# Issuing the merge stage's branch weights from SyncE, round by round, instead of from ScalarE at the stage's head

## The reference

```python
gates = jax.nn.sigmoid(pg.astype(jnp.float32)).astype(dt).reshape(B, T, N_BRANCHES, D_MODEL)
merged = (gates[:, :, 0] * (o_a.astype(dt) @ w_branch_a)
          + gates[:, :, 1] * (o_b.astype(dt) @ w_branch_b)
          + gates[:, :, 2] * (o_c.astype(dt) @ w_branch_c))
x = x + merged @ w_out
u = rmsnorm(x, norm_ffn) @ w_up
...
x = x + (jax.nn.silu(gate) * val) @ w_down
```

## Time and profile before

| what | value |
|---|---|
| time, median of 3 runs | 2480.94 us (2479.97 to 2484.48) |
| the profiled execution's own time | 2482.44 us |
| span of the profiled execution, first to last instruction | 2480.8 us |
| mean granted TensorE clock over the span | 0.948 |
| PE busy | 2253.4 us (91%) |
| DVE busy | 1195.8 us (48%) |
| POOL busy | 673.1 us (27%) |
| ACT busy | 438.8 us (18%) |

### The profile page before, as it was taken

The page is one execution under the profiler, slowest core; times in us unless marked ns, Lnnn a source line. Parts: engine busy times, 40 slices in busy tenths (PEclk is TensorE's granted clock), DMA queues, the critical chain, the costliest instruction groups (busy, mean ns, idle before and its releaser), DMA issues. The chain is left out here.

```text
span 2480.8 us, 46397 instructions
## 1 busy us (share of the span) xinstructions
PE 2253.4 (91%) x19177; PEld 2058.7 (83%) x19177; DVE 1195.8 (48%) x1735; ACT 438.8 (18%) x693; POOL 673.1 (27%) x622
## 2 busy tenths in 40 slices
PE   4999999999999899987787697999999999999986
PEld 3999999888888888864356466989999999999975
DVE  2343443455553143327955262187527735752743
ACT  4001111111110021125743130130000100000022
POOL 3211112333342200002520022334223323432333
PEclk6999999999999999978988798999999999999998
DMA  6112334878885400026662343111111111111113
GB/s 164 49 45 77 133 108 160 260 249 270 261 266 175 163 4 4 4 100 203 224 247 91 115 149 119 43 35 43 41 50 46 39 40 51 43 41 45 47 44 108
DMA packets 256398, 270.14 MB, mean 109 GB/s; under 512 B 24044, under 2 KB 230869, under 8 KB 254508
## 3 DMA queue, kind: packets, MB, share of 16 engines
q1 hardware_dynamic: 214896, 191.93, 24.5%
q10 hardware_dynamic: 33212, 53.18, 6.3%
q0 software_dynamic: 8080, 22.06, 2.6%
HBM read 219.83 MB, written 69.11 MB: 116 GB/s over the span
## 5 line engine op out<-in xcount | busy, mean ns | idle before, releaser
L135 PE MATMUL ps<-ml,fu_wh 128*128 128x352 f32 (+1 forms) x1248 | 410.4, 329 | 22.9 <-POOL fu_wl L129 17.8
L135 PE MATMUL ps<-xl_a,ap_wh 128*128 128x352 f32 (+2 forms) x1200 | 404.7, 337 | 12.4 <-POOL ap_wl L129 12.4
L137 PE MATMUL ps<-mh,fu_wl 128*128 128x352 f32 (+1 forms) x1248 | 409.2, 328 | 0.0
L136 PE MATMUL ps<-mh,fu_wh 128*128 128x352 f32 (+1 forms) x1248 | 409.0, 328 | 0.0
L136 PE MATMUL ps<-xh_a,ap_wh 128*128 128x352 f32 (+2 forms) x1200 | 397.0, 331 | 0.0
L137 PE MATMUL ps<-xh_a,ap_wl 128*128 128x352 f32 (+2 forms) x1200 | 396.7, 331 | 0.0
L129 POOL TENSOR_TENSOR fu_wl<-fu_wt,fu_wh 128x1024 fp32r<-128x1024 f32 (+2 forms) x92 | 201.6, 2192 | 264.6 <-DVE fu_wh L124 264.6
L135 PEld LDWEIGHTS ps<-ml,fu_wh 128*128 128x128 f32 x1248 | 235.9, 189 | 24.8 <-POOL fu_wl L129 24.0
L129 POOL TENSOR_TENSOR ap_wl<-ap_wt,ap_wh 128x1024 fp32r<-128x1024 f32 x50 | 119.7, 2394 | 496.0 <-DVE ap_wh L124 496.0
L135 PEld LDWEIGHTS ps<-xl_a,ap_wh 128*128 128x128 f32 x1200 | 228.0, 190 | 21.1 <-POOL ap_wl L129 13.2
L1079 DVE TENSOR_TENSOR ap_raw<-ps,inv 128x384 f32<-128x384 f32 x150 | 80.4, 537 | 341.7 <-PE ps L137 341.6
(11 more groups left out here) (453 smaller groups left out, 3476.2 us busy)
## 6 DMA issues: line engine op xcount, KB each, us to landing
ap_wt<-in_w_in SPq DMA_DIRECT2D x50, 512.0 KB, 4.0
fu_wt<-in_w_up SPq DMA_DIRECT2D x44, 512.0 KB, 3.7
scr_pj<-ap_raw ACTq DMA_DIRECT2D x39, 544.0 KB, 3.2
out_win_sample<-in_cache_win SPq DMA_DIRECT2D x8, 2040.0 KB
pa<-in_cache_sb_k SPq DMA_DIRECT2D x112, 128.0 KB, 4.8
mg_gate<-scr_pj SPq DMA_DIRECT2D x24, 544.0 KB, 3.6
pa<-in_cache_sb_k POOLq DMA_DIRECT2D x80, 128.0 KB, 5.2
fu_wt<-in_w_down SPq DMA_DIRECT2D x24, 384.0 KB, 3.3
```

What stands on the lines that cost most here:

```text
L135: nc.tensor.matmul(out, wh, xl, start=start, stop=False)
L136: nc.tensor.matmul(out, wh, xh, start=False, stop=False)
L137: return nc.tensor.matmul(out, wl, xh, start=False, stop=stop)
```

## The change

The 24 weight transfers leave ACT's list. SP now issues them, a round at a time: the set for f = 0 at the very beginning, in front of the first gate, and the set for f + 1 right in front of the gate of unit (f, 1). The semaphores and the rule that a transfer of f waits for the one of f - 1 of the same branch stay as they are; it is SP that now waits.

```diff
             @block.sync
             def _(eng):
+                def weights(f):
+                    for i in range(3):
+                        at = slice(first_tile[i], first_tile[i] + 3 - i)
+                        if f:
+                            eng.wait_ge(s_b[i], 16 * f)
+                        eng.dma_start(wb[:, at, f, :], wbr[i][:, :, f, :]).then_inc(s_b[i], 16)
+                weights(0)
                 for n, (f, i) in enumerate(units):
+                    if i == 1 and f + 1 < KT:
+                        weights(f + 1)
                     if n >= NG:
                         eng.wait_ge(s["m"], n - NG + 1)
                     eng.dma_start(gate[:, n % NG, :], g.pj[GATE_TILE - AT + KT * i + f]).then_inc(s_g[n % NG], 16)
...
             @block.scalar
             def _(eng):
-                for f in range(KT):
-                    for i in range(3):
-                        at = slice(first_tile[i], first_tile[i] + 3 - i)
-                        if f:
-                            eng.wait_ge(s_b[i], 16 * f)
-                        eng.dma_start(wb[:, at, f, :], wbr[i][:, :, f, :]).then_inc(s_b[i], 16)
-
                 def rounded(f):
```

## The result

The changed kernel took 2461.78 us (median of 5 runs, 2460.07 to 2468.37) against 2480.94 us before: ratio 0.9922, 95% interval 0.9908 to 0.9936, 19.2 us less. The forecast was 2463.8 us, range 2461 to 2469.

The account below looks back on a forecast made before the run. At the merge's head PE waited for DVE, DVE for ACT's first sigmoid, and that for ACT's weight issues; afterwards PE bounds the stage. 1.7 + 12.95 + 2.4 = 17.1 us off 2480.9 gave 2463.8 us, range 2461 to 2469.

Parts of the forecast that it names:

- PE's start: PE's first product of the merge: first weights land in 2.7 us instead of 4.4, a gain of 1.7 us.
- The idle stretch: PE's wait in the merge between units 1 and 2, for a freed PSUM half: all 12.95 us go.
- What is late next: Gate 1, behind SP's second weights: its sigmoid done by 1401.6 at the latest, needed at 1402.0; no cost to PE.
- the first rival: Merge's head: branch-C weights still take 9.5 us, gate 1's sigmoid comes late; 2464.8 to 2470.0 us, chance 0.13.
- The clock: PE in the merge: without the idle stretch no fall to 1.2 GHz, so the second slow stretch's 2.4 us go.
- the first slow stretch: PE's first 30 half-matmuls of the merge, begun at the 1.2 GHz clock: 3.0 us lost, expected to stay.
- SP's added issues and the tail: 24 issues on SP, about 1.4 us a round, covered by the gates' lead; 8.3 us after PE's last product unchanged: price nothing.
- The block behind: Everything from the next stage's first transfer to the end: moves forward as a block, taking the same time as before.
- The rival that only the issue time is saved: ACT's head in the merge: only 11.4 us of issues saved, PE still idles 1.6 us; 2469.5 us, chance 0.05.

Follow-up runs that it names:

- e3: Changed kernel with all 24 weight issues in one block on SP ahead of the first gate: 2482.09 us, 0.9995 of the kernel before.
- e5: Changed kernel with the first four gates ahead of the first two sets of weights on SP's queue: 2469.20 us.
- e1: Kernel before with weights still issued by ACT, but a round at a time between the sigmoids: 2464.10 us, 0.9920 of before.
- e4: Kernel before with 19 added unused products keeping PE busy between units 1 and 2, where it idled: 2480.11 us, 0.9991 of before.
- e2: Kernel before with a semaphore for each weight transfer, so none of ACT's 24 issues waits for a landing: 2476.85 us.
- e7: Changed kernel with each weight set from f=1 on loaded a second time, into a tile nothing reads: 2458.46 us.

## Why the prediction was right

The direction, the chain and the sum held: 17.1 us were forecast for the merge, 18.0 came (18.7 against the second profile of before, whose merge took 119.5). By the steps:

- **PE's start:** 1.7 us forecast with a landing of 2.7 us; the first weights took 2.5 us, and the gain is 1.9 us (4.46 to 2.59). e3 and e5 show the reason given, the place on the queue.
- **The idle stretch:** all 12.95 us went, as forecast (14.29 us in the second profile of before). e1 shows the cause: sigmoids no longer stand behind 24 issues and landings. Gate 0 took 4.8 to 4.9 us, and its sigmoid was done 7.4 us after the head, inside the 6.3 to 11.5 forecast.
- **What is late next:** unit 1's sigmoid ended at 1400.67 and DVE used it at 1403.74, 3.1 us to spare. The first branch-C weights landed 3.5 us after their issue, not 2.7 and not 9.5; the first rival asked for 9.5.
- **The clock:** 2.4 us forecast; 3.1 us came, the term that was most mis-sized. The 288 halves took 89.99 us against 87.8 at 0.305: the first slow stretch cost 2.2 us where the sum kept 3.0, its value in the earlier trace rows. The second one alone is the 2.1 us of e4. The first one scatters: the first 30 halves took 11.07 to 12.21 us in the five profiles that have them as a row of their own (before twice, e2, e3, e4), 1.9 to 3.1 us above 9.15. So the extra 0.7 us is no work of the change; before's first profile happened to have one of the two longest.
- **SP's added issues and the tail:** nothing, as forecast. Rounds of 10.97 us in the changed kernel and in e7; the tail is 8.28 us against 8.30. The weights' landing beside gates is longer than the 2.7 us of the sum (up to 6.2 us at the head, 3.5 to 4.5 us in steady rounds), but has a round to hide in.
- **The block behind:** the prediction wanted the same time from the next stage's first transfer to the end; the profile had 5.4 us less. Two profiles of before differ by 4.1 us there, a scatter that the prediction did not name, so this shows neither a gain nor its absence.

The rival that only the issue time is saved gave a gain of 11.4 us; the merge gained 18.0, and no idle stretch was left. The prediction split ACT's head into 11.4 us of issues and 14.1 of waits. As prices these did not hold: taking the waits away gave back 8.5 us (e2), because the issues grew.

The Trainium skill's sentence behind this rival ("DMA: Bandwidth & Descriptors", section "Issuing engines are not separate DMA queues") says that issuing from several engines saves only the sequencer's time to initiate a transfer, usually small beside the transfer. e3 agrees with it: the block moved to SP gained 0.5 us. The rival's reading of it, that the change is worth its issues alone, does not hold here: the initiating engine had sigmoids behind the block, and 25.5 us of issues and waits stood in front of the first.

## What to carry to other kernels

Read what an engine does after its transfer issues: a block of issues at a stage's head, each of which waits for a landing, holds back the engine's first real instruction, and here that one freed the buffer that TensorE waited for. Spread such issues in turn with the work that uses them; on both engines tried here that mattered more than the engine (16.3 us of the merge against 1.6). Put the transfer that the bound engine needs first at the front of the queue (1.9 us earlier here), or a stage ahead where an old tile has room (3.1 us of the merge). An idle stretch of TensorE costs its length and a slow start behind it (here 2 to 3 us).

## What was not expected of the hardware

Taking the landing waits away (e2) made the issues themselves longer: 17.0 us for 24, with single ones of 2.4 and 2.9 us while the DMA share was 1.07; in the kernel before, no issue took over 0.51 us. And pauses of PE in the feed-forward part that are the same in every profile drop the clock in some executions and not in others (one to four falls in the four pauses, 1.7 us each), and which ones goes with the moment at which the clock rose over 100 us earlier. Two profiles of the same program differed by 4.1 us in a part where nothing was changed, of which one fall explains less than half.
